# A decoder block and two mixer layers on one core: high parts first in the first chunk behind a norm, and in the first step of the down-projections

## The chip, the core and the metric

One core of a Trainium2 chip runs the whole program in one launch. TensorE (PE) multiplies; VectorE (DVE), ScalarE (ACT) and GpSimd (POOL) make its operands and take its results out of the eight PSUM banks; SyncE (SP) issues the transfers. The metric is device time in microseconds, the median of several runs.

## The reference, cut to what matters

```python
# first block: rms_norm, hybrid mixer, memory attention, then
def squared_relu_mlp(h, w_up, w_down):
    return jnp.square(jax.nn.relu(h @ w_up)) @ w_down
...
# second block, two layers: MLA mixer, then hyena mixer; behind each mixer
        x = layer_norm_2(DEEPNORM_ALPHA * x + m, ln1_g[i], ln1_b[i])
        x = layer_norm_2(DEEPNORM_ALPHA * x + conv_ffn(x, ffn_w_up[i], ffn_w_conv[i], ffn_w_down[i]),
                       ln2_g[i], ln2_b[i])
...
def conv_ffn(x, w_up, w_conv, w_down):
    h = dwconv_centred(x @ w_up, w_conv)
    a, g = jnp.split(h, 2, axis=-1)
    return (jax.nn.silu(g) * a) @ w_down
```

512 tokens, 1024 features, everything in float32. A projection takes as its input the result of a norm, that is, of a sum over all features.

## The kernel before

Activations lie with features on the partitions: a tensor of 1024 features is eight tiles of 128 x 512, and the index of the tile is k. To keep float32 precision with the faster matmul format, each operand is split into a high part (a copy rounded to that format) and a low part (the value less its high part). A product is then three matmuls into the same bank, written by `mm3` (line 136): low weights x high tile, high weights x low tile, high weights x high tile. In the trace `HH` and `HL` are the high and low parts of the input of a projection, `HYH` and `HYL` those of the hyena mixer's result, `MRH` and `MRL` those of the hidden layer `MID` ahead of a down-projection, and `WH` and `WL` (in some chunks a place in `W`) those of the weights. The profile names the moving operand first: `ps<-HH,WL`.

Weights come in chunks of 128 x 2048 (1 MB) in a fixed order: SyncE loads, ScalarE writes WH, GpSimd writes WL, and for a few chunks VectorE writes half of WL (`weights` in its program). A chunk of a projection holds 8 tiles of features by MT = 2 output tiles.

`gemm` runs a projection. For all chunks but the first it goes output tile by output tile. In the first chunk (c == 0) it opens a bank for each of the two output tiles and goes by k, since the tiles come from the norm one after the other: `step` for k waits for `need(k)`, the name under which tile k's low part is announced, and multiplies for both output tiles. Six such first chunks follow a norm or a gate:

- `up` (the MLP of the first block) and `mi` (the input of MLA). `post` makes their tiles: VectorE scales, GpSimd adds the residual, ScalarE writes the high part (tile 0's comes from VectorE), VectorE the low part.
- `fu`, once in each layer (`gemm` with `halves`). Columns 0 to 255 of all tiles first, then columns 256 to 511. The norm ahead of it (`deep_norm`) is split alike, and the second half's statistics are taken meanwhile: `halves(k)` puts onto TensorE column sums behind k = 1 and the spreading of mean and deviation behind k = 3 and k = 5. VectorE turns the column sums into moments before it goes on with the tiles. Low parts 2, 4 and 6 are GpSimd's.
- `hy` (the input of the hyena mixer). `deep_norm_whole` has ScalarE write HH and then X for each tile; both names, `x1` and `hi`, are announced behind the second:

```python
                    act.act(X[:, k, :], X[:, k, :], ACT.Identity, par(g, k), par(b, k)).then_inc(
                        *out(("x1", d, k), ("hn", 4 + d, k, "hi")))
```

- `ho` (the output of the hyena mixer). Its tiles come from a gate, each in two pieces (`hi1`, `hi2`), the low part from VectorE (`hy_low`).

`down` runs a down-projection: eight output tiles in eight banks, which it opens all at its start, and k over the hidden tiles, two to a chunk.

All engines run in the order of the program and wait on counting semaphores; `wait_ge` leaves out a wait that an earlier one covers.

Of the kernel before, what the change touches and what calls it, by code (L numbers as in the profile page):

```python
# [62 lines left out]
CH = {}  # L63
# [188 lines left out]
def build(nc, t):  # L252
# [9 lines left out]
    with es:  # L262
# [16 lines left out]
        up, at, now = V.up, V.at, V.now  # L279
# [175 lines left out]
        def tensor_program(pe):  # L455
# [67 lines left out]
                pe.mm(ps[:], ONE[:], ap, True, True).then_inc(*up(acc, group))  # L523

            def gemm(group, chunks, KT, MT, operand, need, after=None, between=None, base=0, head=True, within=None,
                     halves=None, tail=None):


                def step(ps, m, k, wh, wl, h=None, *sub):
                    col = (k * MT + m) * 128  # L530
# [6 lines left out]
                for c, n in enumerate(chunks):  # L537
                    wh, wl = chunk(n)
                    if c == 0 and halves:
                        ps = [open_bank(group, base + m, hold=True) for m in range(MT)]  # L540
                        for h in range(2):
                            for k in range(KT):
                                for m in range(MT):
                                    ins = step(ps[m], m, k, wh, wl, h, *piece(h))
                                    if h and k == KT - 1:
                                        ins.then_inc(*up(acc, (group, base + m), *[("w_used", n)] * (m == MT - 1)))
                                        close(group, base + m)
                                if h == 0:
                                    halves(k)
# [16 lines left out]
                                tail[1](g, h, True)  # L566
                    elif c == 0 and head:
                        ps = [open_bank(group, base + m, hold=True) for m in range(MT)]
                        for k in range(KT):
                            for m in range(MT):  # L570
                                ins = step(ps[m], m, k, wh, wl)
                                if k == KT - 1:
                                    ins.then_inc(*up(acc, (group, base + m), *[("w_used", n)] * (m == MT - 1)))
                                    if after:
                                        after(base + m)
                                    close(group, base + m)
                            if between and k < KT - 1:
                                between(k)
                    else:
                        for m in range(MT):  # L580
                            g = base + c * MT + m
                            ps = open_bank(group, g)
                            for k in range(KT):
                                ins = step(ps, m, k, wh, wl)
                                if within:
                                    within(g, k)
                            ins.then_inc(*up(acc, (group, g), *[("w_used", n)] * (m == MT - 1)))
                            if after:
                                after(g)
# [291 lines left out]
                if n == 3:  # L881
                    spread("rs", 2, slot=4)

            gemm("up", CH["w_up"], 8, 2, feat, lambda k: ("hn", 2, k), after_up)

            def down(group, chunks, after):

                ps = [open_bank(group, m) for m in range(8)]

                def step(m, k, kk, wh, wl):  # L890
                    col = kk * 1024 + 128 * m
                    pe.wait_ge(*at(group, "in", k))
                    return pe.mm3(ps[m][:], wh[:, col:col + 128], wl[:, col:col + 128], MRH[k % 5][:], MRL[k % 5][:],
                                  k == 0, k == 2 * len(chunks) - 1)

                for c, n in enumerate(chunks[:-1]):
                    wh, wl = chunk(n)
                    for kk in range(2):
                        k = 2 * c + kk
                        for m in range(8):  # L900
                            ins = step(m, k, kk, wh, wl)
                        ins.then_inc(*up(acc, (group, "used", k), *[("w_used", n)] * kk))
                wh, wl = chunk(chunks[-1])
                for m in range(8):
                    for kk in range(2):
                        ins = step(m, 2 * len(chunks) - 2 + kk, kk, wh, wl)
                    ins.then_inc(*up(acc, (group, m), *[("w_used", chunks[-1])] * (m == 7)))
                    if after:
                        after(m)
# [16 lines left out]
                if (n, k) == (5, 0):  # L926
                    spread("nq", slot=12)

            gemm("mi", CH["mla_in"], 8, 2, feat, lambda k: ("hn", 3, k), within=within_in)
            swap("kx", src=KRS[:], need=("krs",))  # L930
            column_sum([(("cvs",), tmp("cq", n), ("cqsq", n), ("cq", n), ("cvs",) if n == 4 else None)
                        for n in (3, 4)])
# [154 lines left out]

            def ffn(l):
                gemm(("fu", l), CH[f"up2_{l}"], 8, 2, feat, lambda k: ("hn", 4 if l == 0 else 6, k),
                     halves=second_half(2 * l))  # L1090
                d = 2 * l + 1
                down(("fd", l), CH[f"down2_{l}"], lambda n: after_deep(d, n))
                square_sums(d, None, 5, 6)
# [18 lines left out]
                if 11 <= n < 19:  # L1112
                    turn_z(0, n - 11)

            gemm("hy", CH["hy_in"], 8, 2, feat, lambda k: ("hn", 5, k), after_hy)

            def to_spectrum(o, m, part, c):
                n = CH["dft_z"][0]
# [11 lines left out]
            for o in range(2):  # L1130
# [34 lines left out]
                if o == 0:  # L1165
# [5 lines left out]
                    turn_z(1, 7)  # L1171
                    to_spectrum(1, 1, 1, 0)
            gemm("ho", CH["hy_o"], 8, 2, lambda k: (HYH[:, k, :], HYL[:, k, :]), lambda k: ("hz", k),
                 lambda n: after_deep(2, n), tail=deep_tail(2))
            ffn(1)

        def scalar_program(act):
# [2046 lines left out]
```

## Time and profile before

| | |
|---|---|
| median of 3 runs | 2192.01 us (2190.08 to 2196.76) |
| the profiled execution | 2187.64 us, its span 2185.8 us |
| TensorE matmul | busy 2094.5 us, 96% of the span, 9729 matmuls |
| VectorE, ScalarE, GpSimd | 59%, 38%, 43% |
| mean granted TensorE clock | 0.965 of full |
| chain that ended last | PE 85%, DVE 9%, ACT 3% |

Busy shares are means over the span. The chain is followed back from the last instruction, each step to what released it. A granted clock of 0.5 is the 1.2 GHz level, 1.0 the 2.4 GHz one. By the timeline the first chunks of `up`, `mi`, `fu`, `hy`, `ho` and `fu` begin about 476, 844, 1083, 1471, 1724 and 1790 us into the span.

### The profile page before, as it was taken

The numbers are of one execution on the slowest core, as the hardware profiler recorded it, in microseconds if no ns is written. First come the engines' busy times: TensorE is split into PE (matmuls) and PEld (weight loads), VectorE is DVE, ScalarE is ACT, GpSimd is POOL, SyncE is SP. The second block draws the span as 40 slices with busy tenths as digits, with TensorE's granted clock in tenths as the row PEclk, the third lists the DMA queues.
The fourth block names the chain that finished last, engine by engine and source line by source line (L and its number), as shares of the span: only waits on it lengthen the run. The fifth ranks groups of instructions, "written<-read, shape, count | busy, mean of one in ns | idle before, by whom it ended". The sixth has DMA issues, their size and how long they took to land.

```text
span 2185.8 us, 23694 instructions
## 1 busy us (share of the span) xinstructions
PE 2094.5 (96%) x9729; PEld 1721.9 (79%) x9729; DVE 1297.7 (59%) x1649; ACT 838.0 (38%) x1207; POOL 938.7 (43%) x404
## 2 busy tenths in 40 slices
PE   8999999989999998999999999999999799999997
PEld 5677768778888887787888888878877688888886
DVE  7766872744235434564387776445678747777644
ACT  4633555551122224676243333233321334333322
POOL 4253135554444445212434444444766544444443
PEclk9999879989999998999899999999999999999998
DMA  5422112212222221111222222214232222222221
GB/s 192 149 101 80 39 39 80 95 58 85 99 98 88 96 101 58 41 41 58 77 78 97 97 97 97 97 58 183 81 113 86 78 78 78 96 97 97 97 97 39
DMA packets 34272, 191.96 MB, mean 88 GB/s; under 512 B 3871, under 2 KB 4463, under 8 KB 14900
## 3 DMA queue, kind: packets, MB, share of 16 engines
q1 hardware_dynamic: 34164, 190.44, 25.0%
q8 instruction: 77, 1.26, 0.2%
q14 instruction: 31, 0.25, 0.0%
HBM read 176.72 MB, written 13.64 MB: 87 GB/s over the span
## 4 chain that ended last, share of the span: by engine, by line
PE 85%; DVE 9%; ACT 3%; POOL 1%; issue 1%; DMA 0%; ACTq 0%; SPq 0%; DVEq 0%; POOLq 0%
PE ps L136 80%; PE ps L135 4%; PE ps L144 1%; DVE ps L171 1%; DVE TMP L159 1%; DVE X L171 1%; DVE X L159 1%; DVE VG L159 1%; DVE YL L159 1%; DVE VG L171 0%; ACT PM L150 0%; DVE HYL L159 0%; ACT PA L153 0%; DVE HL L171 0%; POOL WL L159 0%
## 5 line engine op out<-in xcount | busy, mean ns | idle before, releaser
L159 POOL TENSOR_TENSOR WL<-W,WH 128x2048 fp32r<-128x2048 f32 (+3 forms) x157 | 665.6, 4242 | 958.3 <-ACT WH L152 958.3
L136 PE MATMUL ps<-HH,WL 128*128 128x512 f32 (+1 forms) x1408 | 551.7, 392 | 18.6 <-DVE HL L159 7.6
L136 PE MATMUL ps<-HL,WH 128*128 128x512 f32 (+1 forms) x1408 | 544.8, 387 | 0.0
L136 PE MATMUL ps<-HH,WH 128*128 128x512 f32 (+1 forms) x1408 | 544.7, 387 | 0.0
L152 ACT ACTIVATE WH<-W 128x2048 fp32r<-128x2048 f32 (+2 forms) x148 | 275.2, 1859 | 334.9 <-PE ps L136 327.4
L136 PEld LDWEIGHTS ps<-HH,WL 128*128 128x128 f32 x1408 | 270.2, 192 | 76.7 <-issue 11.8
L136 PEld LDWEIGHTS ps<-HH,WH 128*128 128x128 f32 x1408 | 269.7, 192 | 53.1
L136 PEld LDWEIGHTS ps<-HL,WH 128*128 128x128 f32 x1408 | 270.3, 192 | 51.3 <-issue 0.2
L159 DVE TENSOR_TENSOR MRL<-MID,MRH 128x512 fp32r<-128x512 f32 x76 | 177.4, 2366 | 162.3 <-ACT MRH L152 162.3
L136 PE MATMUL ps<-MRH,WL 128*128 128x512 f32 x608 | 238.2, 392 | 3.3 <-ACT PAD L152 2.2
L136 PE MATMUL ps<-MRH,WH 128*128 128x512 f32 x608 | 236.7, 389 | 0.0
L136 PE MATMUL ps<-MRL,WH 128*128 128x512 f32 x608 | 236.6, 389 | 0.0
L159 DVE TENSOR_TENSOR MID<-TMP,TMP 128x512 f32<-128x512 f32 x44 | 175.8, 3996 | 30.7 <-ACT TMP L153 30.7
L152 ACT ACTIVATE PAD<-ps 128x512 f32<-128x512 f32 x88 | 52.6, 600 | 273.0 <-PE ps L136 273.0
L171 DVE SCALAR_TENSOR_TENSOR TMP<-PAD,PAR,TMP 128x512 f32<-128x512 f32 x176 | 140.8, 800 | 6.3
L136 PEld LDWEIGHTS ps<-MRH,WL 128*128 128x128 f32 x608 | 114.1, 188 | 28.7 <-ACT PAD L152 3.0
L136 PEld LDWEIGHTS ps<-MRH,WH 128*128 128x128 f32 x608 | 114.1, 188 | 24.0
L136 PEld LDWEIGHTS ps<-MRL,WH 128*128 128x128 f32 x608 | 114.2, 188 | 23.5 <-issue 0.5
L159 POOL TENSOR_TENSOR TMP<-TMP,TMP 128x512 f32<-128x512 f32 x47 | 62.2, 1323 | 88.2 <-ACT TMP L153 86.5
L159 DVE TENSOR_TENSOR TMP<-ps,TMP 128x512 f32<-128x512 f32 x36 | 24.9, 690 | 114.9 <-PE ps L136 108.2
L171 DVE SCALAR_TENSOR_TENSOR X<-X,ps 128x512 f32<-128x512 f32 (+1 forms) x36 | 22.6, 628 | 118.3 <-PE ps L136 118.2
L165 DVE TENSOR_SCALAR TMP<-PAD,PAR 128x512 f32<-128x512 f32 x88 | 42.3, 480 | 72.3 <-ACT PAD L152 72.3
(355 smaller groups left out, 3343.7 us busy)
## 6 DMA issues: line engine op xcount, KB each, us to landing
W<-in_up SPq DMA_DIRECT2D x44, 1024.0 KB, 4.8
W<-in_down SPq DMA_DIRECT2D x22, 1024.0 KB, 4.7
W<-in_w_up SPq DMA_DIRECT2D x16, 1024.0 KB, 4.8
W<-in_w_down SPq DMA_DIRECT2D x16, 1024.0 KB, 4.8
W<-in_hy_in SPq DMA_DIRECT2D x12, 1024.0 KB, 4.8
kd<-STG SPq DMA_DIRECT2D x36, 256.0 KB, 2.0
KB<-kd SPq DMA_DIRECT2D x8, 1024.0 KB, 4.9
W<-in_win_ag SPq DMA_DIRECT2D x4, 1024.0 KB, 4.8
```

Source lines behind the costliest of these rows:

```text
L135: return self.eng.matmul(out, lhs, rhs, start=start, stop=stop, skip_group_check=True)
L136: return self.eng.matmul(out, lhs, rhs, start=start, stop=stop)
L144: return QUIET if self.eng is None else self.eng.transpose(out, src, ident)
L152: return self.eng.activation(out, src, fn, scale=scale)
L159: return QUIET if self.eng is None else self.eng.tensor_tensor(out, a, b, op)
L165: return self.eng.tensor_scalar(out, a, s1, None, o1)
L171: return self.eng.scalar_tensor_tensor(out=out, in0=a, scalar=s, in1=b, op0=o1, op1=o2)
```

## The change

`gemm` gets `early`, a function that names the high part of tile k as `need` names the low part. With it, in the first chunk, the two products with the high part (`highs`) wait for that alone and stand one tile ahead of the product with the low part (`lows`). `down` does all high products of its first step ahead of the low ones.

```diff
+                def highs(ps, m, k, wh, wl, h=None, *sub):
+                    col = (k * MT + m) * 128
+                    pe.wait_ge(*at(*early(k), *sub))
+                    p = tokens(h)
+                    pe.mm(ps[:, p], wl[:, col:col + 128], operand(k)[0][:, p], k == 0, False)
+                    pe.mm(ps[:, p], wh[:, col:col + 128], operand(k)[0][:, p], False, False)
+
+                def lows(ps, m, k, wh, h=None, *sub):
+                    col = (k * MT + m) * 128
+                    pe.wait_ge(*at(*need(k), *sub))
+                    p = tokens(h)
+                    return pe.mm(ps[:, p], wh[:, col:col + 128], operand(k)[1][:, p], False, k == KT - 1)
...
                         for h in range(2):
+                            for m in range(MT):
+                                highs(ps[m], m, 0, wh, wl, h, *piece(h))
                             for k in range(KT):
+                                for m in range(MT if k + 1 < KT else 0):
+                                    highs(ps[m], m, k + 1, wh, wl, h, *piece(h))
                                 for m in range(MT):
-                                    ins = step(ps[m], m, k, wh, wl, h, *piece(h))
+                                    ins = lows(ps[m], m, k, wh, h, *piece(h))
...
+                        for m in range(MT if early else 0):
+                            highs(ps[m], m, 0, wh, wl)
                         for k in range(KT):
+                            for m in range(MT if early and k + 1 < KT else 0):
+                                highs(ps[m], m, k + 1, wh, wl)
                             for m in range(MT):
-                                ins = step(ps[m], m, k, wh, wl)
+                                ins = lows(ps[m], m, k, wh) if early else step(ps[m], m, k, wh, wl)
...
-            gemm("up", CH["w_up"], 8, 2, feat, lambda k: ("hn", 2, k), after_up)
+            gemm("up", CH["w_up"], 8, 2, feat, lambda k: ("hn", 2, k), after_up,
+                 early=lambda k: ("hn", 2, k, "hi"))
...
+                def highs(m, k, kk, wh, wl):
+                    col = kk * 1024 + 128 * m
+                    pe.wait_ge(*at(group, "in", k, "hi"))
+                    pe.mm(ps[m][:], wl[:, col:col + 128], MRH[k % 5][:], k == 0, False)
+                    pe.mm(ps[m][:], wh[:, col:col + 128], MRH[k % 5][:], False, False)
...
+                        for m in range(8 if k == 0 else 0):
+                            highs(m, k, kk, wh, wl)
                         for m in range(8):
-                            ins = step(m, k, kk, wh, wl)
+                            ins = step(m, k, kk, wh, wl) if k else lows(m, k, kk, wh)
...
-                 lambda n: after_deep(2, n), tail=deep_tail(2))
+                 lambda n: after_deep(2, n), tail=deep_tail(2), early=lambda k: ("hz", k, "hi2"))
```

`mi`, `hy` and both `fu` get `early` in the same way as `up`. The order of the instructions changes on TensorE alone.

TensorE at the start of `up`, before. `ps6` and `ps7` are the banks of its two output tiles; "waits" names the semaphore, `dve_tile` for what VectorE announces, `act_tile` for ScalarE.

```order
L136 MATMUL ps6<-HH_107,WL0_54 128x512 [waits dve_tile,w_low,w_high]
L136 MATMUL ps6<-HL_108,WH0_52 128x512
L136 MATMUL ps6<-HH_107,WH0_52 128x512
L136 MATMUL ps7<-HH_107,WL0_54 128x512
L136 MATMUL ps7<-HL_108,WH0_52 128x512
L136 MATMUL ps7<-HH_107,WH0_52 128x512
L136 MATMUL ps6<-HH_107,WL0_54 128x512 [waits dve_tile]
L136 MATMUL ps6<-HL_108,WH0_52 128x512
L136 MATMUL ps6<-HH_107,WH0_52 128x512
L136 MATMUL ps7<-HH_107,WL0_54 128x512
L136 MATMUL ps7<-HL_108,WH0_52 128x512
L136 MATMUL ps7<-HH_107,WH0_52 128x512
```

The same place in the change:

```order
L136 MATMUL ps6<-HH_107,WL0_54 128x512 [waits dve_tile,w_low,w_high]
L136 MATMUL ps6<-HH_107,WH0_52 128x512
L136 MATMUL ps7<-HH_107,WL0_54 128x512
L136 MATMUL ps7<-HH_107,WH0_52 128x512
L136 MATMUL ps6<-HH_107,WL0_54 128x512 [waits act_tile]
L136 MATMUL ps6<-HH_107,WH0_52 128x512
L136 MATMUL ps7<-HH_107,WL0_54 128x512
L136 MATMUL ps7<-HH_107,WH0_52 128x512
L136 MATMUL ps6<-HL_108,WH0_52 128x512 [waits dve_tile]
L136 MATMUL ps7<-HL_108,WH0_52 128x512
L136 MATMUL ps6<-HH_107,WL0_54 128x512 [waits act_tile]
L136 MATMUL ps6<-HH_107,WH0_52 128x512
```

Six products for tile 0 behind VectorE's low part stood first; now four with HH stand there, then four more that wait for ScalarE's next high part, and the first two with HL behind those.

TensorE in the first half of the first layer's `fu`, before: the last product of tile 1, the column sums (`ONE` with X and TMP) and the first products of tile 2.

```order
L136 MATMUL ps1<-HH_107,WH1_53 128x256
L135 MATMUL ps5<-ONE_72,X_49 128x1 x2
L135 MATMUL ps6<-ONE_72,TMP1_78 128x1 [waits act_tile]
L135 MATMUL ps6<-ONE_72,TMP1_78 128x1
L136 MATMUL ps7<-HH_107,WL1_55 128x256 [waits pool_tile]
L136 MATMUL ps7<-HL_108,WH1_53 128x256
```

The same place in the change, from the first product with the high part of tile 2 on:

```order
L136 MATMUL ps7<-HH_107,WL1_55 128x256 [waits act_tile]
L136 MATMUL ps7<-HH_107,WH1_53 128x256
L136 MATMUL ps1<-HH_107,WL1_55 128x256
L136 MATMUL ps1<-HH_107,WH1_53 128x256
L136 MATMUL ps7<-HL_108,WH1_53 128x256 [waits dve_tile]
L136 MATMUL ps1<-HL_108,WH1_53 128x256
L135 MATMUL ps5<-ONE_72,X_49 128x1 x2
L135 MATMUL ps6<-ONE_72,TMP1_78 128x1 x2
L136 MATMUL ps7<-HH_107,WL1_55 128x256 [waits act_tile]
```

Ahead of the column sums there now stand the four products with the high part of tile 2, which wait for ScalarE.

TensorE at the start of the down-projection of the first block, in the change: the last three products with the high part `MRH0`, then those with the low part `MRL0`, and the next step in the old order.

```order
L136 MATMUL ps6<-MRH0_151,WH0_52 128x512
L136 MATMUL ps7<-MRH0_151,WL0_54 128x512
L136 MATMUL ps7<-MRH0_151,WH0_52 128x512
L136 MATMUL ps0<-MRL0_156,WH0_52 128x512
L136 MATMUL ps1<-MRL0_156,WH0_52 128x512
L136 MATMUL ps2<-MRL0_156,WH0_52 128x512
L136 MATMUL ps3<-MRL0_156,WH0_52 128x512
L136 MATMUL ps4<-MRL0_156,WH0_52 128x512
L136 MATMUL ps5<-MRL0_156,WH0_52 128x512
L136 MATMUL ps6<-MRL0_156,WH0_52 128x512
L136 MATMUL ps7<-MRL0_156,WH0_52 128x512
L136 MATMUL ps0<-MRH1_152,WL0_54 128x512
```

Before, each of the eight banks got its three products of this step together; the count is the same.

## Rows read from the trace of the kernel before

**Rows 1.** Groups by line of PE: busy, mean ns, idle before and its releasers.

```profile
L136 PE MATMUL ps<-HH,WL 128*128 128x512 f32 (+1 forms) x1408 | 551.7, 392 | 18.6 <-DVE HL L159 7.6 <-DVE HL L171 7.6 <-POOL HL L159 2.4
...
L136 PE MATMUL ps<-HYH,WL 128*128 128x512 f32 (+1 forms) x80 | 29.8, 373 | 5.0 <-DVE HYL L159 4.8
```

**Rows 2.** Timeline, start of `up`: start, us, engine, line, operation, [idle before <-releaser].

```profile
474.59 0.49 DVE L165 TENSOR_SCALAR HH<-X,PAR 128x512 fp32r<-128x512 f32 x1
475.11 0.75 DVE L171 SCALAR_TENSOR_TENSOR HL<-X,PAR,HH 128x512 fp32r<-128x512 f32 x1
...
476.01 0.76 PE L136 MATMUL ps<-HH,WL 128*128 128x512 f32 x1 [2.97 <-DVE HL L171]
...
477.28 0.72 ACT L153 ACTIVATE HH<-X,PAR 128x512 fp32r<-128x512 f32 x1 [2.07 <-DVE X L159]
...
479.86 0.80 PE L136 MATMUL ps<-HH,WL 128*128 128x512 f32 x1 [0.96 <-DVE HL L171]
...
480.46 0.63 PE L136 MATMUL ps<-HL,WH 128*128 128x512 f32 x1
...
480.88 0.63 PE L136 MATMUL ps<-HH,WH 128*128 128x512 f32 x1
```

**Rows 3.** Stretches: width, busy PE, PEld, DVE, ACT, POOL, clock, DMA.

```profile
484.00:485.00 1.00, 1.00 (x6) 0.84 (x5) 1.00 (x2) 0.62 (x1) 1.00 (x2) 0.97 0.00 0
```

**Rows 4.** The chain that ended last, within `up`: start, us, what.

```profile
504.34 152.35 PE ps L136 x672
```

**Rows 5.** Timeline, start of `mi`.

```profile
842.00 1.51 DVE L186 CAST HH<-X 128x512 fp32r<-128x512 f32 x1
...
844.39 0.76 PE L136 MATMUL ps<-HH,WL 128*128 128x512 f32 x1 [3.94 <-DVE HL L159]
...
845.72 0.63 ACT L152 ACTIVATE HH<-X 128x512 fp32r<-128x512 f32 x1 [7.61 <-DVE X L159]
...
848.24 0.79 PE L136 MATMUL ps<-HH,WL 128*128 128x512 f32 x1 [0.96 <-DVE HL L159]
```

**Rows 6.** Timeline, start of `hy`.

```profile
1469.06 0.55 DVE L166 TENSOR_SCALAR HH<-X,PAR 128x512 fp32r<-128x512 f32 x1
...
1470.93 0.77 PE L136 MATMUL ps<-HH,WL 128*128 128x512 f32 x1 [2.71 <-DVE HL L159]
...
1472.79 0.80 ACT L153 ACTIVATE X<-X,PAR 128x512 f32<-128x512 f32 x1
...
1475.00 0.50 PE L136 MATMUL ps<-HH,WL 128*128 128x512 f32 x1 [1.17 <-POOL HL L159]
```

**Rows 7.** Timeline, end of the first chunk of `ho`.

```profile
1736.16 2.10 DVE L159 TENSOR_TENSOR HYL<-VG,HYH 128x256 fp32r<-128x256 f32 x6
1736.27 0.72 ACT L152 ACTIVATE HYH<-VG 128x256 fp32r<-128x256 f32 x2 [1.73 <-DVE VG L159]
...
1736.96 0.50 PE L136 MATMUL ps<-HYH,WL 128*128 128x512 f32 x1 [1.19 <-DVE HYL L159]
...
1738.88 2.41 POOL L159 TENSOR_TENSOR WL<-W,WH 128x1024 fp32r<-128x1024 f32 x1 [5.09 <-ACT WH L152]
...
1741.40 1.22 DVE L159 TENSOR_TENSOR WL<-W,WH 128x1024 fp32r<-128x1024 f32 x1
...
1742.77 0.47 PE L136 MATMUL ps<-HYH,WL 128*128 128x512 f32 x1
```

**Rows 8.** Timeline, first layer's `fu`.

```profile
1084.42 0.51 ACT L153 ACTIVATE HH<-X,PAR 128x256 fp32r<-128x256 f32 x1 [0.63 <-DVE X L171]
...
1085.57 0.58 PE L136 MATMUL ps<-HH,WL 128*128 128x256 f32 x1 [1.39 <-DVE HL L171]
...
1087.02 0.85 PE L135 MATMUL ps<-ONE,X 128*128 128x1 f32 x4
...
1101.87 0.39 PE L136 MATMUL ps<-HH,WL 128*128 128x256 f32 x1 [0.15 <-POOL HL L159]
```

**Rows 9.** Timeline, start of the first layer's down-projection.

```profile
1333.17 0.47 PE L136 MATMUL ps<-MRH,WL 128*128 128x512 f32 x1 [1.10 <-ACT PAD L152]
```

More of the change, by code:

```diff
@@ L525, in gemm @@
             def gemm(group, chunks, KT, MT, operand, need, after=None, between=None, base=0, head=True, within=None,
-                     halves=None, tail=None):
+                     halves=None, tail=None, early=None):
+                def highs(ps, m, k, wh, wl, h=None, *sub):
[9 more added lines that the diff above has]
+                    return pe.mm(ps[:, p], wh[:, col:col + 128], operand(k)[1][:, p], False, k == KT - 1)
                 def step(ps, m, k, wh, wl, h=None, *sub):
@@ L894, in step, with lows @@
                                   k == 0, k == 2 * len(chunks) - 1)
+                def highs(m, k, kk, wh, wl):
[3 more added lines that the diff above has]
+                    pe.mm(ps[m][:], wh[:, col:col + 128], MRH[k % 5][:], False, False)
+                def lows(m, k, kk, wh):
+                    col = kk * 1024 + 128 * m
+                    pe.wait_ge(*at(group, "in", k))
+                    return pe.mm(ps[m][:], wh[:, col:col + 128], MRL[k % 5][:], False, False)
                 for c, n in enumerate(chunks[:-1]):
@@ L927, in within_in @@
                     spread("nq", slot=12)
-            gemm("mi", CH["mla_in"], 8, 2, feat, lambda k: ("hn", 3, k), within=within_in)
+            gemm("mi", CH["mla_in"], 8, 2, feat, lambda k: ("hn", 3, k), within=within_in,
+                 early=lambda k: ("hn", 3, k, "hi"))
             swap("kx", src=KRS[:], need=("krs",))
@@ L1089, in ffn @@
                 gemm(("fu", l), CH[f"up2_{l}"], 8, 2, feat, lambda k: ("hn", 4 if l == 0 else 6, k),
-                     halves=second_half(2 * l))
+                     halves=second_half(2 * l), early=lambda k: ("hn", 4 if l == 0 else 6, k, "hi"))
                 d = 2 * l + 1
@@ L1113, in after_hy @@
                     turn_z(0, n - 11)
-            gemm("hy", CH["hy_in"], 8, 2, feat, lambda k: ("hn", 5, k), after_hy)
+            gemm("hy", CH["hy_in"], 8, 2, feat, lambda k: ("hn", 5, k), after_hy,
+                 early=lambda k: ("hn", 5, k, "hi"))
             def to_spectrum(o, m, part, c):
```

## The prediction

> **What bounds the kernel now.** The groups of instructions by line come first: TensorE is busy for 96% of the span, so only its idle time and its slow stretches can be won. The reader is to see there what ends its idle time ahead of a first product with HH or HYH: 18.6 us over the whole run, nearly all ended by a writer of HL, and 5.0 us ended by HYL [rows 1]. That is 23.6 us, and it is all that the change can touch: about 1% of the time. The timeline at the start of `up` shows the form of it. The matmul starts at 476.01, 0.15 us after the low part of tile 0 ends (475.11 + 0.75 = 475.86), but the high part had ended at 474.59 + 0.49 = 475.08. After six matmuls the array waits again and resumes at 479.86, though tile 1's high part was ready at 477.28 + 0.72 = 478.00 [rows 2]. Two paces matter: 0.42 us from start to start in that stretch (480.46 to 480.88) and 152.35/672 = 0.227 us later [rows 2, 4]. The granted clock says why: it is 0.97 of full in the microsecond from 484 on [rows 3], where the matmuls ahead of it came at nearly twice the pace's time. So the stage begins at the 1.2 GHz level and changes to the 2.4 GHz one about 4.1 us after the array resumed.
>
> **What the change does to a chunk.** No instruction is added, none removed on any engine: per tile and output tile there are still three products. Only their order on TensorE differs, and what they wait for. The old order asks for low 0, then low 1, and so on. The new one asks for high 0 (4 matmuls), high 1 (4), low 0 (2), high 2 (4), low 1 (2). Two things follow, and I price each place by them. At the start, four matmuls begin earlier, and the next gap ends when high 1 is there instead of low 1; the new order then has 44 matmuls left against 42. With D the time by which the array resumes earlier, the gain at one unchanged pace p is D - 2p. At the end, two matmuls follow the last low part instead of six or more.
>
> The level of the clock gives each place two ends. If it rises at the same moment of the program as before, the early time is spent at the slow pace and the gain is (D/0.42 - 2) x 0.227. If it rises the same time after the array resumes, the gain is D - 2 x 0.227. I take a value between, since rows of one execution can't tell them apart.
>
> **The terms.**
> - `up`: resumes at 478.00 + 0.15 = 478.15 instead of 479.86, D = 1.71. Ends 0.47 and 1.26. The pace of the vector operations that make the tiles caps the upper one: I take **0.8**.
> - `mi`: tile 1's high part ends at 845.72 + 0.63 = 846.35, so 846.50 instead of 848.24, D = 1.74; ends 0.49 and 1.29 [rows 5]. Its first high part, a cast that ends at 843.51, is hardly ahead of the first matmul at 844.39, but the first burst isn't what decides. I take **0.9**.
> - `hy`: here ScalarE writes HH and then X, and one increment behind the second covers both. High 1 thus counts at 1472.79 + 0.80 = 1473.59, and the array resumes at 1473.74 instead of 1475.00, D = 1.26. In the rows before, the matmul at 1475.00 lasts 0.50 us against 0.80 at 479.86: the level was already up when it resumed [rows 2, 6]. If it still is, the gain is 1.26 - 0.45 = 0.8. But the first burst of the new order is four matmuls at 1469.06 + 0.55 + 0.15 = 1469.76, done by 1471.5, and a gap of 2.3 us follows (before: six from 1470.93, a gap near 1.2 [rows 6]). If the level then rises only 4.1 us after 1473.74, as `up` did [rows 2, 3], 9.8 matmuls run at 0.42 and lose 0.19 each: 0.8 - 1.9 = -1.1. I take **0.2**.
> - `ho`: makes its tiles slower than the array uses them, so the end counts. From 1736.96 the old order had 18 matmuls (tiles 5 to 7), the new has 10 (low 5, high 7, low 6, low 7), the high part of tile 7 being there at 1736.27 + 0.72 and the last low one at 1736.16 + 2.10 = 1738.26. That is 8 x 0.227 = 1.8 us. The next chunk, however, started at 1742.77 behind the VectorE half of its low weights (1741.40), which stands behind a residual that follows the array and moves up; the GpSimd half ends at 1738.88 + 2.41 = 1741.29 and does not [rows 7]. So 1742.77 becomes 1741.45: **1.3**. Lower end 0.5, if the gaps, which the shorter work makes longer, cost clock.
> - `fu`, two layers, in halves of 256 columns, paces half as long (estimate: 0.21 and 0.11). In the second half the array waits for nearly each low part; at the end, two matmuls stand behind the last low part instead of six or twelve: from 1101.87 on twelve ran, and eight fewer are 0.9 us [rows 8]. But in the first half the column sums at 1087.02 stand behind tile 1, and the new order puts high 2 ahead of them: 12 matmuls from 1084.42 + 0.51 + 0.15 = 1085.08 instead of 6 from 1085.57. At 0.21 they come 0.8 us later, at 0.11 0.2 us later. VectorE waits for them with the moments, and behind those stand its scalings, ScalarE's high and GpSimd's low parts of the second half: the delay goes into the end. So 0.1 and 0.7; in rows the first layer runs this at the slow pace, the second partly. Sum of both **1.0**, ends 0 and 1.8.
> - The three down-projections: **0**. The diff splits their first step, but all eight banks are opened ahead of it, and the wait of 1.10 us at 1333.17 is for a bank that ScalarE's PAD copy frees (one row of three such) [rows 9]. Both parts of MID's tile 0 were made long before, so nothing waits for either, and 24 matmuls stay 24.
>
> **More waits.** A tile has two waits now instead of one. A satisfied one shows no gap in the 672 matmuls at 0.227 [rows 4], which hold such waits only at chunks; the nearest one that is just released is the 0.60 us spacing at 479.86 instead of 0.42 [rows 2]. Such waits are likely only where the array waits anyway. I add nothing, and keep 0.5 us for the range.
>
> **Sum.** 0.8 + 0.9 + 0.2 + 1.3 + 1.0 + 0 = 4.2 us. The profiled execution took 2187.64 us (span 2185.8), so it would be 2183.4; it lay 4.4 us under the median of 2192.01 that the three runs show, so the median becomes 2187.8. The lower ends sum to 0.47 + 0.49 - 1.1 + 0.5 + 0 - 0.5 = -0.1, the upper to 1.26 + 1.29 + 0.8 + 1.35 + 1.8 = 6.5. Everything behind a chunk follows the array (chain of waits: 672 matmuls on end behind `up` [rows 4]), so I expect no loss later.
>
> **One rule against it.** Rows first: in the old order a bank gets three products, then the other bank three, and from 1101.87 or 476.01 on this shows no loss but the clock's [rows 2, 8]. The new one changes banks after two, then after each one. The Trainium skill, "TensorE: Matmul & The Clock Gate", section "A second HAM failure mode: psum-queue depth-cycling", says that going round PSUM banks leaves small pauses by which the clock swings between its levels. By that the six chunks would lose, the last rival below; no run here shows it yet.
>
> **The rivals.**
> - *More than counted.* The clock rises with the array and `fu` keeps both 0.9 us: 6.5 us and a little from earlier tiles, about 2185. For it: the level in `up` came only after the second gap. Against: `hy`, where the earlier order already had it. Chance 0.2.
> - *The idle time only moves.* The array starts earlier and waits longer for high 1, the clock rises when it did, and `fu` gives its end back through the column sums. Left are `ho` 1.3 and some tenths: 1.5 us, 2190.5. For it: the fixed-moment ends above, and a gap of 2.3 us in `hy`. Chance 0.2.
> - *Slower.* The short bursts and the changes of bank keep the lower level for the whole chunk. A chunk of 48 has some 32 matmuls at the fast pace; at 0.42 they cost 32 x 0.19 = 6 us. Two places cost 12, which outweighs 4.2 by more than 0.3%; three give 18 - 4 = 14 us, 2206. It decides from the second place on. Against: in `ho` the array idles 1.19 us ahead of 1736.96 and the matmul there still lasts 0.50 us, as at the higher level in `hy` [rows 6, 7]. Chance 0.04.
> - That the change does nothing is true of the down-projections, and counted.
>
> **How the numbers follow.** Forecast 0.56, the rivals 0.2, 0.2 and 0.04. About 0.3% (6.6 us) is what a measurement can tell from no change here. The forecast and the second rival lie within it, the first rival at its edge: faster 0.19, same 0.77, slower 0.04. The runs before spread over 6.7 us, so the range is the sum of the ends (2185.5 to 2192.1) widened by some 2 us: 2183.5 to 2193.5.
>
> **What the changed profile would show.** The first matmul of `up` and `mi` 0.7 to 0.8 us closer behind the last column sums, four of them, and a gap ended by ScalarE's HH and not by HL. HYL still ends waits in `ho`, with the next chunk about 1.3 us sooner, ended by GpSimd's WL. In `fu` the column sums later and the moments with them, but the second half shorter. The same 1.1 us ahead of the down-projections. Idle time with HH and HYH as a whole falls by less than the time won where the clock rises earlier. Wrong if the level is low in the middle of a first chunk, or if a new wait stands ahead of the chunk behind.

## The result: slower by a quarter of a per cent

| | before | changed |
|---|---|---|
| median, 22 runs each | 2191.35 us (2184.70 to 2197.89) | 2197.20 us (2191.13 to 2204.28) |
| ratio | | 1.0025, 95% interval 1.0014 to 1.0035 |
| profiled execution: span, clock | 2185.8 us, 0.965 | 2194.0 us, 0.963 |

The forecast was 4.2 us faster and a range up to 2193.5. It came out some 5.5 us slower, outside the range. By the bound of 0.3% it is still "same".

These rows of the changed kernel answer [rows 1]; columns as there:

```profile
L136 PE MATMUL ps<-HH,WL 128*128 128x512 f32 (+1 forms) x1408 | 553.0, 394 | 16.2 <-ACT HH L153 5.7 <-DVE HH L165 2.2 <-DVE HH L186 2.1
...
L136 PE MATMUL ps<-HYH,WL 128*128 128x512 f32 (+1 forms) x80 | 29.6, 370 | 1.2 <-DVE WL L159 1.2
...
L136 PE MATMUL ps<-HYL,WH 128*128 128x512 f32 (+1 forms) x80 | 27.8, 366 | 3.3 <-DVE HYL L159 3.3
```

HL has gone from the first row and HYL from the second; together they are 17.4 us against 23.6. But HYL now ends 3.3 us of waits at the low products, which had none before, so the idle time at these products fell by 2.9 us only, from 23.6 to 20.7. The waits of the changed kernel (us in total, times, longest) name new ones. Of the first row here, 1.9 us (one wait) were there before; the other three rows are new, and the last two are part of the 17.4:

```profile
PE ps L135 <- POOL TMP L159: 2.9, 2, 1.9
...
PE ps L135 <- DVE Y L159: 2.6, 1, 2.6
...
PE ps L136 <- ACT X L153: 1.9, 1, 1.9
...
PE ps L136 <- DVE WL L159: 1.2, 1, 1.2
```

**The chunks began as forecast.** Timeline of the changed kernel at the start of `up`, which answers [rows 2]:

```profile
470.72 0.49 DVE L165 TENSOR_SCALAR HH<-X,PAR 128x512 fp32r<-128x512 f32 x1
...
471.35 0.77 PE L136 MATMUL ps<-HH,WL 128*128 128x512 f32 x1 [2.18 <-DVE HH L165]
...
473.42 0.72 ACT L153 ACTIVATE HH<-X,PAR 128x512 fp32r<-128x512 f32 x1 [2.06 <-DVE X L159]
...
474.19 0.80 PE L136 MATMUL ps<-HH,WL 128*128 128x512 f32 x1 [0.79 <-ACT HH L153]
```

From tile 0's high part to the second burst it is 474.19 - 470.72 = 3.47 us; before, 479.86 - 474.59 = 5.27 [rows 2]. Both gaps of the changed kernel end with a high part, as forecast. The next chunk (`ps<-HH,W`) starts at 486.66, which is 15.94 us behind that high part; before it was 491.46 - 474.59 = 16.87:

```profile
486.66 0.39 PE L136 MATMUL ps<-HH,W 128*128 128x512 f32 x1
```

From that high part on, the chunk is 0.9 us shorter.

**Where it was lost.** The chain that ended last gives places that both kernels have. Of the changed kernel (start, us, what):

```profile
439.29 24.51 PE ps L136 x108
...
657.55 163.46 PE ps L136 x720
...
917.34 13.43 PE ps L136 x59
...
1337.08 116.93 PE ps L136 x512
...
1463.00 11.35 PE ps L135 x64
...
1547.76 5.48 PE ps L136 x24
```

The stretches between these starts are the stages below: `up` from the x108 to the x720, `mi` on to the x59, `fu` (first layer) on to the x512, and `hy` from the x64, the column sums of its norm, to the x24. `ho` and the second `fu` follow in the same way, with the chain's starts at 1684.66, 1750.63 and 2047.66. The same places of the kernel before start at 442.37, 657.76, 912.47, 1333.17, 1458.98, 1540.01, 1676.56, 1742.77 and 2039.53.

| stage, us | before | changed | difference |
|---|---|---|---|
| `up` | 215.39 | 218.26 | +2.9 |
| `mi` | 254.71 | 259.79 | +5.1 |
| `fu`, first layer | 420.70 | 419.74 | -1.0 |
| `hy` | 81.03 | 84.76 | +3.7 |
| `ho` | 66.21 | 65.97 | -0.2 |
| `fu`, second layer | 296.76 | 297.03 | +0.3 |

`up`, `mi` and `hy` lose 11.7 us. The whole profiled execution is only 8.2 us longer, in the main because `up` begins 3.1 us sooner in it (439.29 against 442.37) and the first `fu` is 1.0 shorter. That start is no effect of the change: over the fourteen profiled executions of this document it scatters from 434.6 to 444.8 us. So single profiles are compared by stage here, and whole times by their medians.

What happened in `up` is in the timeline of the changed kernel:

```profile
485.36 9.46 DVE L159 TENSOR_TENSOR Y<-Y 128x512 f32<-128x512 f32 x7
...
486.92 1.92 ACT L152 ACTIVATE WH<-W 128x2048 fp32r<-128x2048 f32 x1 [1.73 <-PE ps L136]
...
488.91 4.57 POOL L159 TENSOR_TENSOR WL<-W,WH 128x2048 fp32r<-128x2048 f32 x1 [5.01 <-ACT WH L152]
...
494.88 1.05 PE L135 MATMUL ps<-ONE,Y 128*128 128x1 f32 x8 [2.62 <-DVE Y L159]
```

and in its chain:

```profile
488.26 0.70 DVE Y L159
...
488.99 5.05 DVE Y L159
...
494.13 0.70 DVE Y L159
```

`Y<-Y` are VectorE's seven additions of squares for the next norm's sum; the column sums `ONE,Y` wait for the last. The others take about 0.7 us each. The one that starts at 488.99, 0.08 us after GpSimd has started on the low weights, lasts 5.05 and ends 0.56 us behind them. The column sums come 2.62 us late. The kernel before had the same work in another order of time:

```profile
489.21 5.12 DVE L159 TENSOR_TENSOR Y<-Y 128x512 f32<-128x512 f32 x7
...
493.71 5.05 POOL L159 TENSOR_TENSOR WL<-W,WH 128x2048 fp32r<-128x2048 f32 x1 [5.96 <-ACT WH L152]
```

There the weights came 4.50 us behind the first addition, when the seven were nearly through, and here 3.55 us. It was close even then: the last of the seven had started only 0.08 us ahead of GpSimd's operation, and that time GpSimd was the one held up, with 5.05 us instead of 4.57. From the kernel before:

```profile
493.63 0.69 DVE L159 TENSOR_TENSOR Y<-Y 128x512 f32<-128x512 f32 x1
```

Those weights can be made when the first chunk has freed its buffer (`w_used`), so the earlier end of the chunk calls them earlier. Behind the wait the clock fell too: in stretches of 1 us (columns as in [rows 3]) of the changed kernel

```profile
496.00:497.00 1.00, 1.00 (x3) 0.73 (x3) 0.18 (x1) 0.23 (x1) 0.00 (x0) 0.52 1.00 426
498.00:499.00 1.00, 1.00 (x4) 0.81 (x3) 0.00 (x0) 0.00 (x0) 0.00 (x0) 0.50 0.00 0
500.00:501.00 1.00, 1.00 (x6) 0.82 (x5) 0.00 (x0) 0.00 (x0) 0.00 (x0) 1.00 0.00 0
```

where the kernel before has 1.00 in each.

In `mi` it is the third chunk's low weights and VectorE's last step on the rotary angle. Changed kernel:

```profile
861.04 4.89 POOL L159 TENSOR_TENSOR WL<-W,WH 128x2048 fp32r<-128x2048 f32 x1 [4.93 <-ACT WH L152]
...
861.50 4.72 DVE L166 TENSOR_SCALAR ANG<-ANG 128x512 f32<-128x512 f32 x1
...
866.25 0.63 ACT L153 ACTIVATE SN<-ANG 128x512 f32<-128x512 f32 x1 [3.98 <-DVE ANG L166]
...
873.58 2.39 PE L135 MATMUL ps<-ONE,TMP 128*128 128x1 f32 x16 [1.04 <-POOL TMP L159]
```

Kernel before:

```profile
861.49 0.43 DVE L166 TENSOR_SCALAR ANG<-ANG 128x512 f32<-128x512 f32 x1
...
862.21 4.60 POOL L159 TENSOR_TENSOR WL<-W,WH 128x2048 fp32r<-128x2048 f32 x1 [6.11 <-ACT WH L152]
```

There it missed by 862.21 - 861.92 = 0.29 us; now the weights come 1.2 us sooner against VectorE's step. Then ScalarE's sine waits 3.98 us, its copies for the column sums stand behind the sine, GpSimd squares such a copy, and TensorE waits 1.04 us for the square. The clock falls behind this wait as well: it is 0.50 in the slices 875:876, 879:880 and 907:908, where the kernel before has 1.00.

The Trainium skill, "SBUF — State Buffer", section "SBUF: two separate sides", has this: VectorE and GpSimd share a pair of ports, which a VectorE operation takes when it has two inputs in SBUF and GpSimd's operation reads SBUF too, or when it runs in a mode that uses two ports; whichever starts first holds the pair to its end while the other blocks. The rows agree on the additions, which have two inputs, both ways round: 5.05 instead of 0.70 us where GpSimd's was first, and GpSimd's 5.05 instead of 4.57 where VectorE's was. The step on the angle has one input, and it took 4.72 instead of 0.43 beside one of 4.89; no row shows in what mode it ran.

### The profile page after: what moved, and what is told of

It is laid out like the page before. It is cut to its first block, busy times and chain, and to the rows that moved or that the text cites. A ratio compares the mean times of both kernels' runs of the same rounds, so it can differ in the third digit from the quotient of the medians.

```text
span 2194.0 us, 23694 instructions
## 1 busy us (share of the span) xinstructions
PE 2099.3 (96%) x9729; PEld 1724.7 (79%) x9729; DVE 1307.9 (60%) x1649; ACT 837.3 (38%) x1207; POOL 939.4 (43%) x404
## 4 chain that ended last, share of the span: by engine, by line
PE 83%; DVE 9%; ACT 4%; POOL 2%; issue 1%; DMA 1%; SPq 0%; ACTq 0%; DVEq 0%; POOLq 0%
PE ps L136 78%; PE ps L135 4%; PE ps L144 1%; POOL X L159 1%; DVE TMP L159 1%; DVE X L171 1%; DVE X L159 1%; DVE VG L159 1%; DVE ps L171 1%; DVE YL L159 1%; POOL WL L159 1%; DVE VG L171 0%; DVE Y L159 0%; ACT WH L152 0%; ACT PM L150 0%
## 5 line engine op out<-in xcount | busy, mean ns | idle before, releaser
L159 POOL TENSOR_TENSOR WL<-W,WH 128x2048 fp32r<-128x2048 f32 (+3 forms) x157 | 666.0, 4245 | 961.3 <-ACT WH L152 961.3
L136 PE MATMUL ps<-HL,WH 128*128 128x512 f32 (+1 forms) x1408 | 534.5, 387 | 0.0
L136 PEld LDWEIGHTS ps<-HH,WL 128*128 128x128 f32 x1408 | 271.2, 193 | 75.3 <-ACT HH L153 10.2
L159 DVE TENSOR_TENSOR MRL<-MID,MRH 128x512 fp32r<-128x512 f32 x76 | 177.4, 2366 | 162.4 <-ACT MRH L152 162.4
L159 DVE TENSOR_TENSOR MID<-TMP,TMP 128x512 f32<-128x512 f32 x44 | 161.3, 3665 | 30.7 <-ACT TMP L153 30.7
L171 DVE SCALAR_TENSOR_TENSOR TMP<-PAD,PAR,TMP 128x512 f32<-128x512 f32 x176 | 158.5, 900 | 6.3
L159 POOL TENSOR_TENSOR TMP<-TMP,TMP 128x512 f32<-128x512 f32 x47 | 62.2, 1323 | 93.4 <-ACT TMP L153 91.8
L159 DVE TENSOR_TENSOR TMP<-ps,TMP 128x512 f32<-128x512 f32 x36 | 24.8, 690 | 116.8 <-PE ps L136 108.5
L177 DVE RECIPROCAL SM<-SM 128x4 f32<-128x4 f32 (+1 forms) x36 | 6.2, 174 | 127.7 <-ACT SM L153 112.3
```

What stands on the lines that cost most here:

```text
L136: return self.eng.matmul(out, lhs, rhs, start=start, stop=stop)
L159: return QUIET if self.eng is None else self.eng.tensor_tensor(out, a, b, op)
L171: return self.eng.scalar_tensor_tensor(out=out, in0=a, scalar=s, in1=b, op0=o1, op1=o2)
L177: return QUIET if self.eng is None else self.eng.reciprocal(out, src)
```

## The experiments

Each ran 12 times beside 35 runs of the kernel before; its profiled execution gives the stages. In kernels with two lines more, L159 is L161.

**Parts of the change.** Against the changed kernel, e1 and e2 keep `early` in one call, e4 in all but two:

```diff
-            gemm("up", CH["w_up"], 8, 2, feat, lambda k: ("hn", 2, k), after_up,
-                 early=lambda k: ("hn", 2, k, "hi"))
+            gemm("up", CH["w_up"], 8, 2, feat, lambda k: ("hn", 2, k), after_up)
...
```

So in e2, e4, e5, e6 and e12; the other calls are undone in the same way, and in e1, e2, e5, e6 and e12 the down-projections' first step as well.

*Up alone:*

> The new order in the first chunk of up alone; the other five chunks and the down-projections as before. Theory A (the chunk ends earlier, so GpSimd's 4.6 us of low weights start earlier and land on VectorE's additions of squares, which the column sums behind the next chunk wait for): an addition of some 5 us, the first column sum of this statistic waiting about 2.6 us, the clock falling there, and the kernel 2 to 3 us slower than before. Rival B (the order itself costs clock inside the chunk): the chunk is longer than before, no wait at the column sums. Rival C (the loss of the whole change came from chance in the clock): 0.8 us faster.

Measured: 2192.66 us, ratio 1.0017 (0.9999 to 1.0034). The additions 9.47 us, the column sums waiting 2.6, stage `up` +2.8: theory A. Beyond its own stage, `mi` took 1.4 us more although its collision was absent; all four kernels with the collision in `up` alone (e1, e6, e9, e12) show that, 256.1 to 256.3 us. In each of them the clock is low once more late in `mi` (0.50 in 907:908 of e1, 1.00 there in the kernel before). Why a wait in `up` brings that is not shown.

*Mi alone:*

> The new order in the first chunk of mi alone. Theory A: GpSimd's low weights for the third chunk start about 1.2 us earlier, hold VectorE's last step on the angle for 4.7 us instead of 0.4, ScalarE's sine and its copies for the column sums follow 2.8 us later, TensorE waits about 1 us at them and the clock falls: about 5 us slower than before. Rival B: the chunk itself is longer. Rival C: 0.9 us faster.

Measured: 2193.36 us, 1.0008 (0.9992 to 1.0025). The angle 4.71 us, the sine waiting 3.97, stage `mi` +3.3, below the 5 expected. The mechanism is there, the size forecast for it was too large, and the times alone don't tell it from nothing.

*All but up and mi:*

> The new order everywhere but in up and mi. Theory A: the loss is that of up and mi, so what is left is hy, ho, both fu and the down-projections: between 2 us faster and 3 us slower than before, the loss if any from the clock in hy. Rival B (the order costs clock wherever it stands): 3 to 5 us slower than before.

Measured: 2193.20 us, 1.0015 (0.9995 to 1.0035). `up` and `mi` as before, the first `fu` -1.0, `hy` +3.7. The times alone don't show a loss, but `hy` has one that theory A doesn't explain. Its profile lost 4.6 us more in and behind the second `fu`: 2.0 us in the stage and 2.6 behind it. The part behind it stands in e6 and e7 too (2.3 and 2.6), and 1.6 us of it in e10, which has the old order in `fu`. In these four the column sums of the last norm take 10.2 to 11.3 us instead of 8.8, much like those ahead of `hy`. The changed kernel and e3, with the new order in the second `fu`, don't show this loss.

**The collisions taken away, the order kept.** GpSimd waits for VectorE at two chunks, nothing else:

```diff
+BEHIND = {CH["w_up"][2]: ("hacc", 2, 7), CH["mla_in"][2]: ("angle",)}
...
+                    if i in BEHIND:
+                        pool.wait_ge(*at(*BEHIND[i]))
                     pool.wait_ge(*at("w_high", i))
```

> The whole change, and GpSimd starts the low weights of the third chunk of up only behind the last addition of squares, those of the third chunk of mi only behind the angle. No instruction more. Theory A: the additions take 0.7 us each again and the angle 0.4 us, the waits of 2.6 and 1.0 us at the column sums go, and the kernel is 6 to 8 us faster than the changed kernel, that is 0 to 4 us faster than before. Rival B or C: no different from the changed kernel, 5 us slower than before.

Measured: 2188.67 us, 0.9991 (0.9975 to 1.0007). Its timeline:

```profile
486.29 5.12 DVE L161 TENSOR_TENSOR Y<-Y 128x512 f32<-128x512 f32 x7
...
491.48 4.59 POOL L161 TENSOR_TENSOR WL<-W,WH 128x2048 fp32r<-128x2048 f32 x1 [6.66 <-DVE Y L161]
...
493.51 0.95 PE L137 MATMUL ps<-ONE,Y 128*128 128x1 f32 x8
```

Both waits are gone, `up` takes 215.05 and `mi` 254.94 us. Against the changed kernel the ratio falls by 0.34%, some 7 us, the two intervals don't overlap, and the two waits are all that differs. Theory A holds for `up` and `mi`. `hy` still takes 84.72.

**The collisions put into the kernel before.** TensorE's order is the old one:

```diff
+                    if (s, k) == (2, 5):
+                        dve.wait_ge(*at("w_high", CH["w_up"][2]))
                     dve.tt(Y[:, 0, :], Y[:, 0, :], Y[:, k, :], ALU.add).then_inc(*out(("hacc", s, k)))
...
+                if P == 128:
+                    dve.wait_ge(*at("w_high", CH["mla_in"][2]))
                 dve.ts(arg, arg, PI_IN, -PI_IN, ALU.min, ALU.max).then_inc(*out(*names))
```

> The kernel before with the order of TensorE untouched. VectorE waits for the high weights of the third chunk ahead of the fifth addition of squares in up and ahead of the last step on the angle in mi, so that both start when GpSimd starts its 4.6 us of low weights; the waits by themselves move them by 1.6 and 0.7 us, which nothing in the trace of before follows at once. Theory A (the two engines' operations exclude each other): one addition and the step on the angle last 4 to 5 us, the column sums wait 2 to 3.5 us and 1 us, 5 to 8 us slower than before. Rival B or C (the loss belongs to the order of TensorE or to chance): both operations 0.4 to 0.7 us, time within 1 us of before.

Measured: 2192.13 us, 1.0023 (1.0006 to 1.0039), that is 5 us at the ratio. Timeline:

```profile
493.61 4.57 POOL L159 TENSOR_TENSOR WL<-W,WH 128x2048 fp32r<-128x2048 f32 x1 [5.99 <-ACT WH L152]
493.63 6.61 DVE L159 TENSOR_TENSOR Y<-Y 128x512 f32<-128x512 f32 x3 [1.70 <-ACT WH L152]
...
500.30 1.24 PE L135 MATMUL ps<-ONE,Y 128*128 128x1 f32 x8 [3.34 <-DVE Y L159]
```

The last three additions take 6.61 us, one of them 5.09, the angle 4.85. The collision costs this without any new order. Stage `up` is +5.3, `mi` only +0.3, and the first `fu`, untouched, is 2.5 shorter. Around the first chunk of that `fu` the clock was low for 6.8 us, against 13.7 in the seven other profiles with the old order there. So what such a wait costs in one execution also hangs on the clock behind it.

**What is left: hy.** With the old order in `fu`, the granted clock falls 4.6 to 5.2 us behind the start of the column sums ahead of `hy` (worked out from the mean of the slice in which it falls); with the new one, 2.0 to 2.8. First the kernel before, whose sums start at 1458.98, then the changed one, from 1463.00:

```profile
1462.98:1463.98 1.00, 1.00 (x10) 1.00 (x10) 0.57 (x2) 0.00 (x0) 1.00 (x1) 0.85 0.06 16
```

```profile
1465.00:1466.00 1.00, 1.00 (x9) 1.00 (x8) 0.00 (x0) 0.11 (x1) 1.00 (x2) 0.71 0.00 0
```

0.85 puts the fall 0.7 us into its slice, 4.7 behind the start; 0.71 puts it at 2.4. The 64 small matmuls of the sums then take 11.35 us instead of 9.26. The clock also comes back later, 22.9 us behind the start of the sums instead of 15.0. Which edit moves it?

e5 has the new order in `hy` alone, e6 in both `fu` and `ho`, e12 in the first `fu`:

```diff
-                     halves=second_half(2 * l), early=lambda k: ("hn", 4 if l == 0 else 6, k, "hi"))
+                     halves=second_half(2 * l), early=(lambda k: ("hn", 4, k, "hi")) if l == 0 else None)
```

> The new order in the first chunk of hy alone. In the three profiled runs so far that had it, the stage from the column sums of its norm to the end of the projection took 84.7 us against 81.0, and the clock fell 2.3 us earlier within those column sums, ahead of the chunk. Theory H (the new order in hy costs it: high part counted only behind X, a gap of 1.9 us or more, the clock low for longer): 3 to 4 us longer here too. Rival F (it comes from the fu stage ahead, whose new order leaves another phase of the clock at the column sums): this stage as before within 1 us.

Measured: 2194.12 us, 1.0018 (1.0002 to 1.0033). Stage `hy` 81.49, +0.5, the fall at 4.8. Kernels with the old order in `fu` and `hy` show 81.0 to 81.7 (before, e1, e2, e8, e10, e11), so even the 0.5 isn't shown to be the order's. Timeline:

```profile
1469.67 0.77 PE L136 MATMUL ps<-HH,WL 128*128 128x512 f32 x1 [1.52 <-DVE HH L166]
...
1473.57 0.79 PE L136 MATMUL ps<-HH,WL 128*128 128x512 f32 x1 [1.85 <-ACT X L153]
```

Rival F: `hy`'s own order isn't the 3.7 us. But the interval of the times lies above 1 while the profiled span equals that of before (2185.8). One execution can't show what the others lost; that stays open.

> The new order in both fu and in ho, the rest as before. The first fu stage 1.0 us shorter as in the three runs that had it, ho and the second fu between 1 us shorter and 0.5 us longer. Theory H: hy as before, so the kernel 1 to 2 us faster. Rival F: the clock falls earlier in the column sums of the norm ahead of hy and its stage is 2 to 4 us longer, the kernel 1 to 3 us slower.

Measured: 2188.99 us, 1.0003 (0.9987 to 1.0019). First `fu` 419.84, `hy` 84.99 with the old order in `hy`: rival F by the stage, though the time shows no loss. And in this kernel with the old order in `up` the collision was there. It hit the last of the seven additions, which took 4.95 us:

```profile
490.59 9.37 DVE L159 TENSOR_TENSOR Y<-Y 128x512 f32<-128x512 f32 x7
...
494.85 4.57 POOL L159 TENSOR_TENSOR WL<-W,WH 128x2048 fp32r<-128x2048 f32 x1 [5.72 <-ACT WH L152]
```

> The new order in the first chunk of fu in the first layer alone. Theory F (it shortens its own stage by 1 us and moves the fall of the clock in the column sums ahead of hy): stage of fu 0.9 to 1.0 us shorter, fall 2.5 to 2.8 us after the start of the column sums, hy stage 3.7 to 4.0 us longer, the kernel 2 to 3 us slower than before. Rival: the hy stage as before, 1 us faster.

Measured: 2193.70 us, 1.0011 (0.9998 to 1.0024). `fu` -0.8, fall at 2.8, but `hy` only 82.75, +1.7: the clock rose again some 16.5 us behind the start of the sums, not 22.9 as in the changed kernel. Direction as expected, size half. The additions took 9.37 us here too, which is part of its time.

*Is it only a shift in time?* The kernel before, with ten matmuls more in the first layer's down-projection:

```diff
+                            if group == ("fd", 0) and (k == 6 or k == 8 and m < 2):
+                                col = kk * 1024 + 128 * m
+                                ins = pe.mm(ps[m][:], wl[:, col:col + 128], MRL[k % 5][:], False, False)
```

It adds products of low by low, which the others leave out.

> The kernel before, with ten products more of low weights by low part (128 x 512, 2.27 us at the fast pace) in the down-projection of the first layer, 80 to 100 us ahead of the column sums of the norm ahead of hy. Nothing else moves. So far the clock fell 4.7 to 5.2 us after the start of those column sums where fu was old and 2.5 to 2.8 us after it where fu was new, five runs each. Theory P (only the place in time counts: the fall follows something that lies ahead of the down-projection, and what is moved against it meets it elsewhere): the fall comes at another place, near 2.6 us after the start, the stage from there to the end of hy 3 to 4 us longer, the kernel 5 to 6 us slower. Rival T (the light column sums themselves bring the fall about after a fixed time, and the new fu changes something else): fall at 4.9 us as before, the kernel 2.3 us slower.

Measured: 2196.19 us, 1.0024 (1.0011 to 1.0037). The sums start at 1457.94, and, counted from there, the slice in which the clock falls is two us earlier than in the kernel before:

```profile
1459.94:1460.94 1.00, 1.00 (x10) 1.00 (x9) 0.00 (x0) 0.11 (x1) 1.00 (x2) 0.83 0.00 0
```

The fall is at 2.7, the stage 1542.91 - 1457.94 = 84.97 us, +3.9. This is theory P: 2.27 us of full work elsewhere came with the whole loss of `hy`, with every order as before, in the one profile there is. The fall doesn't follow from the light sums alone. The additions of squares were hit here too (one of 4.99 us), so not all of the slower time belongs to `hy`. Why the new `fu`, which makes the sums 1 us earlier, ends at the same place is open.

**What a better version would be.**

> The kernel before, with the two low weights of GpSimd behind VectorE's additions and angle and nothing else. In the run with the new order in fu and ho alone the additions of squares lasted 9.37 us although up was unchanged, so the kernel before has the collision too in some executions. Theory A with that: 0 to 2 us faster than before, at most the chance of the collision by its 3 to 5 us. Rival (never there in the kernel before): no change.

Measured: 2188.97 us, 0.9989 (0.9977 to 1.0001); the kernel before with `BEHIND`. It can't be told from no change, but the collision exists in it: of the seven profiled executions with the old order in `up` and no counter-measure (before, e2, e4, e5, e6, e9, e12) three had it, of the two with the new order (changed, e1) both. What the three share is the clock ahead of the chunk: in them it rose 4.6 to 4.7 us behind tile 0's high part, in the other four 9.4 to 9.6. Their first chunk was 0.2 to 0.3 us shorter (16.62 to 16.67 against 16.86 to 16.94), which is more than the 0.08 us by which the kernel before escaped. The rows thus point to the shorter chunk as what brings the collision, by the new order or by the clock.

> The new order in up, mi, ho and both fu and in the down-projections, hy as before, and GpSimd's two low weights behind the last addition of squares and behind the angle. Theory A with H: nothing is lost any more, 2 to 4 us faster than before. A with F: hy keeps a loss of 2 to 4 us, the kernel within 1 us of before.

Measured: 2186.28 us, 0.9986 (0.9972 to 0.9999), `hy` 85.00 with the old order in it: as A with F says for the stage, but 3 us faster than before where that case said within 1.

> The new order in up, mi, ho and the down-projections, fu and hy as before, the two low weights of GpSimd behind VectorE's work. Theory (fu costs the hy stage 3.7 us by the clock, more than the 1 us that it gains): the hy stage as before, up 0.3 and ho up to 0.3 us shorter, 1 to 3 us faster than before. Rival: fu's gain counts and no other, the kernel as before within 0.5 us.

Measured: 2185.67 us, 0.9977 (0.9963 to 0.9991), `hy` 81.55. The fastest of all, 5 us at the ratio, though not told apart from e7. It is clear of 1, but `BEHIND` is part of it: against e11, which has `BEHIND` alone, no gain of the order is shown.

## Why the prediction was wrong

**The step that failed** is "Everything behind a chunk follows the array (...), so I expect no loss later." Weights follow it as well. The end of a first chunk frees a weight buffer, ScalarE and then GpSimd start at once, and GpSimd's 4.6 us exclude VectorE. Taking the two collisions out of the changed kernel gave back some 7 us by the ratios (e3); putting them into the old order cost some 5 (e8). The rows to see it were there in the trace of the kernel before: the low weights 0.29 us behind the end of the angle and 0.08 us behind the start of the last addition. The prediction looked at GpSimd's low weights only in `ho`, and even there not at what VectorE does beside them.

**Term by term.**
- `up` 0.8: the chunk gained 0.9, the stage lost 2.9. The 0.9 is in part the clock's: in the changed kernel, e1, e7 and e10 the chunk takes 15.92 to 15.94 us and the clock rises 8.1 to 8.3 us behind tile 0's high part; in e3 it rises after 9.5, as in the kernel before, and the chunk takes 16.43, a gain of 0.44. That is the prediction's lower end, 0.47, for a rise at the same moment. Without the collision the stage was 0.3 us shorter in e3 and 1.6 in e7 and e10. The changed kernel and e1 have the chunk and the clock of e7 and e10, and their stage is 4.4 to 4.5 us longer: that is what the collision costs.
- `mi` 0.9: the chunk's end moved up 1.2 against VectorE's step, the stage lost 5.1. Without the collision +0.2 (e3) and -0.7 (e7, e10).
- `hy` 0.2, ends -1.1 and 0.8: alone -0.5 in its profile, inside, and inside the scatter of the old order as well. The mechanism of the lower end came true in part: the array resumed at 1473.57 behind ScalarE's X and the clock rose about 3.8 us later. The 3.7 us that the stage lost in the changed kernel came from ahead of the chunk, for which the prediction had no term: e6 and e7 have the old order in `hy` and lost 4.0.
- `ho` 1.3: -0.2 in the changed kernel, no gain on the whole over the six profiles with it. The step "So 1742.77 becomes 1741.45" failed by the same exclusion. Changed kernel:

```profile
1747.03 2.37 POOL L159 TENSOR_TENSOR WL<-W,WH 128x1024 fp32r<-128x1024 f32 x1 [5.09 <-ACT WH L152]
1748.17 2.32 DVE L159 TENSOR_TENSOR WL<-W,WH 128x1024 fp32r<-128x1024 f32 x1
...
1750.63 0.47 PE L136 MATMUL ps<-HYH,WL 128*128 128x512 f32 x1 [1.20 <-DVE WL L159]
```

  VectorE's half moved up as forecast, into GpSimd's half, and took 2.32 us instead of 1.22 [rows 7]: 2.30 to 2.33 in all six profiles with the new order in `ho`, 1.22 in the eight without.
- `fu`, both 1.0: the first alone gained 0.8 to 1.0 in its stage, in six of six profiles, more than forecast for it. The clock has a part in it: around this chunk it is low for 10.2 us in all six, for 13.7 in seven of the eight others. The second shows nothing clear: +0.3 here, and its stage scatters from -4 to +2 us over the runs, with either order. The column sums did come behind twelve matmuls. Not foreseen: behind the first `fu` the clock falls earlier in the sums ahead of `hy`, in six of six profiles, at 1.7 to 4.0 us.
- Down-projections 0: right. The changed kernel waits 0.99 us at 1337.08 for the same copy:

```profile
1337.08 0.47 PE L136 MATMUL ps<-MRH,WL 128*128 128x512 f32 x1 [0.99 <-ACT PAD L152]
```

**The rivals.** The "Slower" one had the right sign and the wrong place: `up` reached the fast pace within its chunk and was shorter. Only the chunk of `hy` was at the low level for much longer than before, for its first 10 us instead of 3. In e6, e7 and e9, which have the old order there, it was so for some 9 us: the changes of bank are not the reason. What the array itself gained can't be told from these times: e10 against e11, that is `up`, `mi`, `ho` and the down-projections, is 0.12% or 2.6 us, where the terms sum to 3.0, but from the two intervals its uncertainty is some 4 us either way (an estimate), and the 1.3 for `ho` in that sum was wrong.

## What to carry to other kernels

When a stage gets shorter, list what its end releases on every engine, and lay each released operation of GpSimd over what VectorE does at that time: if VectorE's result is waited for, one microsecond gained can cost five. A margin of tenths of a microsecond between a 4.6 us GpSimd operation and a short VectorE one is a danger sign, and a wait that puts the long one behind costs nothing that could be measured here (e11, 0.9989), where its result is needed later. Gains of 1 us behind which the array does light work can be outweighed by where the clock falls there; such edits are judged by the stages behind them in several profiles.

## What was not expected of the hardware

- A VectorE operation of 0.43 to 0.70 us lasted 4.7 to 5.1 us beside a GpSimd subtraction of 128 x 2048 (4.6 to 4.9 us), in nine cases in seven profiled executions; it also holds for VectorE's subtraction of 1.22 us beside GpSimd's of 2.37.
- The granted clock fell at one of two places in the same column sums, 4.6 to 5.2 or 2.0 to 2.8 us behind their start, in seven and seven profiles. Six of the seven early falls came with the new order in the first `fu`, some 370 us ahead; the seventh came with 2.27 us more of full work some 80 to 95 us ahead. How either sets the place of the fall is open.
